# One program part for each layer: the meeting of the engines moves from behind the mixers to behind the first four gathers of the experts' results

## The reference

```python
for l in range(DEPTH):                       # 2
    h = rms_norm(x, norm_mix_g[l])
    # four mixers A..D on u = h @ W_in, each 256 wide: neighbourhood attention,
    # bidirectional mLSTM, conformer convolution, grouped-query attention
    proj = einsum('bsnc,ncd->bsnd', branches, w_branch)     # four branches, 256 -> 1024
    g = sigmoid(h @ w_gate + b_gate)                        # four gates of 1024
    x = x + sum_n(g * proj) @ w_out
    h = rms_norm(x, norm_ffn_g[l])
    x = x + moe(h)          # best of 4 groups, two of its 4 experts, gated MLP, 16 experts
y = rms_norm(x, final_norm_g)
```

## Time and profile before

| | |
|---|---|
| median of 3 runs | 2101.95 us (2100.12 to 2103.16) |
| the profiled execution, its time | 2105.18 us |
| its span, first to last instruction | 2103.3 us |
| busy: PE, DVE, ACT, POOL | 95%, 49%, 25%, 17% |
| mean granted clock of TensorE | 0.981 |
| DMA, mean | 173 GB/s |

### The profile page before, as it was taken

How to read it: one execution, slowest core, us unless ns; L and a number is a source line. 1 busy time by engine, 2 the same in 40 slices (tenths; PEclk the granted TensorE clock), 3 DMA queues, 4 the chain that set the end, 5 groups by cost and what they waited for, 6 DMA issues and landing times. The chain is left out here.

```text
span 2103.3 us, 24261 instructions
## 1 busy us (share of the span) xinstructions
PE 1996.2 (95%) x8820; PEld 1257.0 (60%) x8820; DVE 1037.7 (49%) x1898; ACT 527.4 (25%) x1126; POOL 351.5 (17%) x278
## 2 busy tenths in 40 slices
PE   7999999999998999999599999999999999999991
PEld 4555656555555556888455556645555655578871
DVE  3588516353544876111275883344534469641114
ACT  2233312445330001111123332134454200111111
POOL 2322220111120012000233222102112100210003
PEclk9999999999999999999899999999999999999996
DMA  5555648111217406998641211211221273279965
GB/s 217 187 202 222 248 191 320 55 71 70 81 61 296 161 21 230 392 399 310 225 187 40 86 71 56 81 50 66 105 81 45 83 280 124 91 290 418 373 229 190
DMA packets 67398, 362.97 MB, mean 173 GB/s; under 512 B 5809, under 2 KB 6193, under 8 KB 54065
## 3 DMA queue, kind: packets, MB, share of 16 engines
q1 hardware_dynamic: 42656, 278.57, 34.5%
q10 hardware_dynamic: 17712, 57.68, 6.9%
q0 software_dynamic: 6912, 25.17, 3.2%
HBM read 250.24 MB, written 112.20 MB: 172 GB/s over the span
## 5 line engine op out<-in xcount | busy, mean ns | idle before, releaser
L736 PE MATMUL bank<-hT,ring 128*128 128x384 f32 x1056 | 359.7, 490 | 2.9 <-ACT gbuf L927 2.9
L736 PE MATMUL bank<-x,ring 128*128 128x384 f32 x1056 | 359.7, 490 | 1.2 <-POOL ring L1244 1.2
L736 PEld LDWEIGHTS bank<-hT,ring 128*128 128x128 f32 x1056 | 195.6, 190 | 152.3 <-issue 29.9
L736 PEld LDWEIGHTS bank<-x,ring 128*128 128x128 f32 x1056 | 195.0, 190 | 143.0 <-issue 21.7
L1058 DVE SCALAR_TENSOR_TENSOR reg_a<-cvx,pp,reg_a 128x783 f32<-128x783 f32 x120 | 142.8, 1190 | 4.3
L900 ACT ACTIVATE sums<-bank 128x384 f32<-128x384 f32 x132 | 64.9, 491 | 289.0 <-PE bank L736 287.9
L714 PE MATMUL bank<-ring,hT 128*128 128x272 f32 (+1 forms) x384 | 127.9, 493 | 0.0
L1036 DVE SCALAR_TENSOR_TENSOR gbuf<-bank,sums 128x384 f32<-128x384 f32 x96 | 53.5, 558 | 136.0 <-PE bank L736 105.9
L1856 DVE SCALAR_TENSOR_TENSOR prob<-prob,bank 128x256 f32<-128x256 f32 x30 | 12.6, 421 | 202.0 <-ACT prob L1630 202.0
L714 PEld LDWEIGHTS bank<-ring,hT 128*128 128x128 f32 x384 | 72.5, 190 | 51.6 <-issue 43.7
L1602 ACT ACTIVATE prob<-x 128x1024 f32<-128x1024 f32 x12 | 12.7, 1059 | 335.2 <-DVE x L1733 335.2
(11 more groups left out here) (282 smaller groups left out, 3116.2 us busy)
## 6 DMA issues: line engine op xcount, KB each, us to landing
ring<-in_wd SPq DMA_DIRECT2D x26, 2048.0 KB, 8.4
blocks<-hT SPq DMA_DIRECT2D x16, 3072.0 KB, 21.1
gate_dram<-gbuf ACTq DMA_DIRECT2D x64, 384.0 KB, 2.3
ring<-gate_dram SPq DMA_DIRECT2D x16, 1536.0 KB, 6.9
wide<-in_we SPq DMA_DIRECT2D x8, 2048.0 KB, 12.9
oT<-in_we SPq DMA_DIRECT2D x8, 2048.0 KB, 12.7
reg_b<-in_we SPq DMA_DIRECT2D x8, 2048.0 KB, 12.1
ring<-in_we SPq DMA_DIRECT2D x8, 2048.0 KB, 14.0
```

Source lines behind the costliest of these rows:

```text
L736: mm = nc.tensor.matmul(bank[i % 2][:, 0:HALF], w[:, k, :], a[:, k, :], start=(k == 0 and r in (0, 1, 3)), stop=(k == 3), skip_group_check ...
```

## The change

Each part becomes one layer, head, mix and tail, and the final norm is a part of its own. The meetings stand now at the end of a layer's tail. Of the twelve gathers that fetch the experts' results, the four of tiles 0 and 1 are issued ahead of the meeting, the other eight behind it. Because no meeting orders the branch stage behind the mixers any more, explicit waits do it, and the branch units start at bank 2 (bank 0 and 1 hold the last gate product). The loads of the branch stage are spread over its units, and `wr_k` moves behind the 64 units.

```diff
+EARLY = 2
@@ head_gpsimd
-            for t in range(T):
+            for t in range(EARLY, T):
                 for c in range(TOP):
                     gather(pool, t, c)
@@ tail
-            out_bank = (0, 1, 0, 2, 1, 0, 3)
+            branch_bank = lambda q: bank[(q + 2) % 8]
+            out_bank = (2, 3, 2, 0, 3, 2, 1)
@@ tail_sync
+            def load_x(sp):
...
+            def tail_sync(sp):
+                sp.wait_ge(proj_mm, units_of["proj"])
+                sp.wait_ge(turn_mm, units_of["turn"])
+                load_gates(sp, layer, 1)
+                sp.dma_start(wr_sb, wr[layer]).then_inc(wr_in, 16)
+                sp.dma_start(gain_row, ffn_in[layer:layer + 1, :].to_broadcast([P, D])).then_inc(ffn_row_in, 16)
+                sp.wait_ge(gates_back[1], 16 * (KD // 2 * layer + 1))
+                load_branch(sp, layer, 1)
                 for m in range(2, KD):
                     sp.wait_ge(gated, 8 * (m - 1))
                     load_gates(sp, layer, m)
-                    if m == 5:
+                    if m == 2:
+                        load_out(sp, 1)
+                    elif m == 3:
+                        load_x(sp)
+                    elif m == 5:
                         load_out(sp, 0)
@@ tail_tensor
+                pe.wait_ge(turn_ev, units_of["turn"])
+                pe.wait_ge(mlh_done, units_of["ml"])
                 for q, (m, n, hf) in enumerate(units):
                     pe.wait_ge(wb_in[m // 4], 16 * (layer + 1))
                     if q >= 8:
                         pe.wait_ge(gated, q - 7)
+                    elif branch_bank(q) is bank[0]:
+                        evicted(pe, units_of["proj"] - 1)
@@ tail_gpsimd, its end
+                for t in range(EARLY):
+                    for c in range(TOP):
+                        gather(pool, t, c)
@@ tail_vector
-                dve.wait_ge(wr_in, 16)
-                done(tt(wr_k, wr_k, pp[:, PP_GFFN:PP_GFFN + KD].unsqueeze(2).to_broadcast([P, KD, NG + NE]), ALU.mult),
-                     wr_done)
...
                 halves(0)
                 halves(1)
+                dve.wait_ge(wr_in, 16)
+                done(tt(wr_k, wr_k, pp[:, PP_GFFN:PP_GFFN + KD].unsqueeze(2).to_broadcast([P, KD, NG + NE]), ALU.mult),
+                     wr_done)
@@ stretch, on PE; the other engines alike
-                    if layer:
-                        tail_tensor(pe)
                     if layer < L:
                         head_tensor(pe, layer)
                         mix_tensor(pe, layer)
+                        tail_tensor(pe)
```

More of the change, by code:

```diff
@@ L1361, in tail_sync @@
                     sp.dma_start(x[:, 2:6, :], x_sample.rearrange("b (t p) d -> p (b t) d", p=P)).then_inc(x_back, 16)
-                load_out(sp, 1)
+            def tail_sync(sp):
[6 more added lines that the diff above has]
+                load_branch(sp, layer, 1)
                 for m in range(2, KD):
@@ L1414, in tail_tensor @@
                         pe.wait_ge(gated, q - 7)
+                    elif branch_bank(q) is bank[0]:
+                        evicted(pe, units_of["proj"] - 1)
                     for k in range(2):
-                        mm = nc.tensor.matmul(bank[q % 8][:, 0:HALF],
+                        mm = nc.tensor.matmul(branch_bank(q)[:, 0:HALF],
                                               wb_sb[m // 4][:, n, k, (m % 4) * P:(m % 4 + 1) * P],
@@ L1710, in tail_vector @@
                     to, tmp = mT[:, m, half[hf]], dg[:, 0, 0:HALF]
-                    done(stt(tmp if n else to, gate, 1.0, bank[q % 8][:, 0:HALF], ALU.add, ALU.mult), gated)
+                    done(stt(tmp if n else to, gate, 1.0, branch_bank(q)[:, 0:HALF], ALU.add, ALU.mult), gated)
                     if n:
@@ L1893, in stretch @@
         def stretch(layer):
-            if layer:
-                tail_sync, tail_tensor, tail_scalar, tail_gpsimd, tail_vector = tail(layer - 1)
+            if layer < L:
+                tail_sync, tail_tensor, tail_scalar, tail_gpsimd, tail_vector = tail(layer)
             with nc.Block() as block:
@@ L1899, in _ @@
                 def _(sp):
-                    if layer:
-                        tail_sync(sp)
                     if layer == L:
@@ L1906, in _ @@
                         mix_sync(sp, layer)
+                        tail_sync(sp)
                 @block.tensor
                 def _(pe):
-                    if layer:
-                        tail_tensor(pe)
                     if layer < L:
@@ L1914, in _ @@
                         mix_tensor(pe, layer)
+                        tail_tensor(pe)
                 @block.scalar
                 def _(act):
-                    if layer:
-                        tail_scalar(act)
                     if layer == L:
@@ L1925, in _ @@
                         mix_scalar(act)
+                        tail_scalar(act)
                 @block.gpsimd
                 def _(pool):
-                    if layer:
-                        tail_gpsimd(pool)
                     head_gpsimd(pool, layer)
@@ L1933, in _ @@
                         mix_gpsimd(pool, layer)
+                        tail_gpsimd(pool)
                 @block.vector
                 def _(dve):
-                    if layer:
-                        tail_vector(dve)
                     head_vector(dve, layer)
@@ L1941, in _ @@
                         mix_vector(dve, layer)
+                        tail_vector(dve)
         first, last = min(layer_sems), max(layer_sems)
```

## The result

The changed kernel takes 2105.45 us (median of 20 runs, 2103.2 to 2106.95), the kernel before 2101.26 (20 runs, 2098.49 to 2103.44) in the same comparison. The ratio is 1.0019, 95% interval 1.0012 to 1.0025: some 4 us slower, where I forecast 2096.2 and a range of 2091 to 2102. The profiled execution took 2105.43 us with a span of 2103.6.

What follows compares the result with a forecast made beforehand. PE, busy 95% of the span, was taken as the bound, so its idle or slow stretches count. 12.6 - 0.6 - 6.2 = 5.8 us less takes the median from 2101.95 to 2096.2 us, range 2091 to 2102.

Steps and rivals of the forecast that it cites:

- The step to the branch stage: From last gate product to output projection: PE's idle, stall and low clock go, gaining 7.7 us in layer 0, 4.9 in layer 1.
- `wr_k`, cost 0.6: Behind the 64 units, `wr_k` delays DVE's third addition to `x` and PE's turn, some 0.3 us in each layer.
- The loads at 0: Branch stage: spread loads cost PE nothing; bounds 0 and 4.6 us for both layers.
- The rival of the late output half: Branch stage: output half 1 lands in 24.3 us, costing PE 2.3 us a layer, 2100.7 us; chance 0.15.
- The meeting at the layer's end: Behind the fourth gather: drain, meeting and restart make the power of tile 0 3.1 us late in each layer.
- so I take the 2.0 us: Layer's end: POOL's drain assumed to last 2.0 us past the fourth gather, as layer 1's drain outlasted POOL's last operation.
- the drain waits for the landing: Rival, layer's end: drain lasts until the fourth gather lands, 6.2 us after issue; power 6.3 late, 2102.5 us; chance 0.12.
- its slow form: Rival, layer's end: same wait with the slowest landing, 8.5 us; power 8.6 us late a layer, 2107.1 us; chance 0.06.
- The bound that I gave from above: Layer's end: drain's extra time at most the fourth gather's landing, 6.2 us after its issue, at most 8.5.
- My test in the trace: Layer's end: forecast wrong if the fifth gather starts within 2 us of the fourth's end or more than 5 after.

Runs made afterwards that it cites:

- drain alone: Kernel before with only a POOL drain added behind the fourth gather, no meeting there: 2111.23 us, ratio 1.0044.
- no gather ahead: Changed kernel with all twelve gathers issued behind the meeting at the layer's end: 2096.68 us, ratio 0.9976.
- no POOL drain: Changed kernel with POOL not drained at a part's end and the second meeting made by semaphores alone: 2091.31 us, ratio 0.9951.
- `wr_k` alone: Kernel before with only `wr_k` moved behind the 64 units, meeting and loads as they were: 2100.18 us, ratio 0.999.
- bunched loads: Changed kernel without POOL's drain at the meetings, all branch-stage loads issued at the stage's start as before: 2097.03 us, ratio 0.998.
- no POOL drain, `wr_k` at 39: Changed kernel without POOL's drain at the meetings, `wr_k` behind unit 39 instead of behind the 64 units: 2090.17 us, ratio 0.9943.
- six gathers ahead: Changed kernel with six gathers, not four, issued ahead of the meeting: 2107.12 us, timed once.
- before, no POOL drain: Kernel before, meetings where they were, POOL not drained and the meeting between parts made by semaphores alone: 2101.49 us, ratio 1.0003.

## Why the prediction was wrong

The three measures account for every run within its interval. Branch is the sum of both layers minus 182.1 us, turn is 0.35 us a layer where `wr_k` stands behind the units, power is the sum of both layers minus 23.7 us, the mean of four traces of before.

| | branch | turn | power | sum | measured |
|---|---|---|---|---|---|
| changed kernel (two traces) | -11.8 | +0.7 | +13.8 | +2.7 | +4.0 (+2.5 to +5.3) |
| drain alone | -0.8 | 0 | +9.4 | +8.6 | +9.2 (+5.9 to +12.8) |
| no gather ahead | -11.8 | +0.7 | +5.5 | -5.6 | -5.0 (-7.1 to -2.7) |
| no POOL drain | -11.8 | +0.7 | +0.1 | -11.0 | -10.3 (-13.0 to -7.4) |
| `wr_k` alone | -3.1 | +0.7 | -0.3 | -2.7 | -2.1 (-4.0 to -0.2) |
| bunched loads | -6.0 | +0.7 | -0.5 | -5.8 | -4.2 (-6.1 to -1.9) |
| no POOL drain, `wr_k` at 39 | -11.8 | 0 | 0 | -11.8 | -12.0 (-14.9 to -9.0) |
| six gathers ahead | -11.8 | +0.7 | +15.8 | +4.7 | +6.0, timed once |
| before, no POOL drain | -1.4 | 0 | +0.1 | -1.3 | +0.6 (-1.5 to +2.5) |

The measured column is the ratio minus one, times 2101.5. Every sum lies inside its interval where there is one. Eight of the nine lie below the measured value, though, by 0.9 us in the mean of all nine: the four traces of before may lie that much off a usual execution, or a small term is missing; no run tells which. The branch stage took 85.14 or 85.15 us in both layers of all the versions with the new order and spread loads.

- **The step to the branch stage, gain 12.6.** Right: no idle time, no stall, full clock, the units in 82.9 us in both layers. The size was read from one execution, where it was 13.3 by start times; over four it is 11.8. The parts of it do not add up one by one: `wr_k` alone gives 3.1 us, 2.9 more come when the meeting goes as well (bunched loads, 6.0), and 5.8 more when the loads are also spread.
- **`wr_k`, cost 0.6.** Right: 0.35 us a layer, gained back by the move to unit 39.
- **The loads at 0.** Right for the changed kernel, where PE does not stand once in the units. The rival of the late output half did not occur. The bunched version shows what the spreading is worth once PE runs freely, 5.8 us; my text saw a possible cost in it, not that the gain rests on it.
- **The meeting at the layer's end, cost 6.2. This is the step that failed**, with the words "so I take the 2.0 us". The drain behind four gathers lasts 8.8 to 9.9 us. It ends 0.7 to 1.0 us after the last landing, as do the two behind six gathers. The cost is 13.4 us in the profiled trace and 14.3 in the second, against the mean of before. I had put this as the rival "the drain waits for the landing" at 12.6 us and 2102.5, with a chance of 0.12, and its slow form at 17.2 us. What happened lies at the first of the two, since the fourth gather landed in 5.5 to 6.3 us, not in 8.5. GPSIMD Engine Reference of the Trainium skill, "2.1 Instruction dispatch", which I weighed and set aside, says that a POOL instruction that writes is complete when its data has landed. It does not speak of drains or gathers. The gathers' own rows here end 0.94 us after their start, long before the landing, but the drain behind them ends as the page's rule, taken over to it, has it.
- **Why I chose wrongly.** I took the size from layer 1's drain behind the mixers, 2.0 us longer than POOL's last operation. No gather was in flight there, so the row could not show a wait for one: 24 indirect transfers had gone since the drain before, and by the count above the 2.0 us are theirs. That gathers follow each other without waiting for a landing counted in my mind against a wait of the drain; it only shows that the queue runs ahead. The bound that I gave from above, the landing, was the value, with 0.7 to 1.0 us on top.

The rival's sum came to 0.6 us more than before, measured are 4.0. The later power adds 1.2 to it (13.8 against 12.6), the smaller gain 0.8 (11.8 against 12.6), `wr_k` 0.1. That makes the 2.7 of the table; the 1.3 us that are left lie inside the interval, and no run settles them.

The result lies outside the range, since I had left a fifth of the chance beyond it, most of it on just this rival and its slow form. My test in the trace was the right one: the fifth gather starts 7.1 us after the fourth's end, beyond the 5 us that I had named.

## What to carry to other kernels

Put no drain, and no meeting that drains POOL, behind its indirect transfers where work on the path is queued on POOL behind it: here it waited for their landings, and all that was queued came late. If a meeting must stand there, either hold the transfers back behind it (9 us better here) or make it by semaphores alone (14 us better here) and let the readers wait for the transfers' own semaphores. When a stall is removed, look for what it had covered, and read a gain from several executions: a low clock ahead of the stall cost nothing, behind it 1.7 us. Where a change has several parts, take them away one at a time: the spread loads looked like a detail and carry half of the gain.

## What the runs showed of the hardware

- A drain of POOL waits for the data of its indirect transfers, though the transfers' rows on POOL last 0.94 us each: drains of 8.8 to 9.9 us behind four gathers, 11.2 and 11.3 behind six, 1.1 and 2.0 with none under way.
- A drain with no transfer under way is not free either: its length went with the number of indirect transfers since the drain before, 0.07 us with 0, 0.58 with 6, 0.74 with 8, 1.06 with 12, 2.02 to 2.06 with 24. The 2.0 us of the forecast came from such a drain, with 24.
- Without its drain, POOL's sequencer passes two meetings and the clearing between them while its gathers are still queued (1024.4 against a fourth gather at 1025.99), and the power of tile 0 comes as early as in the kernel before (+0.1 us for both layers).
- The 2.40 us of idle on PE behind the mixers were followed by 3.4 us at the lower clock at once in both layers of the runs with `wr_k` alone and with the drain alone, and in one layer of three of the four traces of before; elsewhere it came behind DVE's stall or not at all. Why it comes when it does, no run shows.
